# Two weight rings moved to the far end of SBUF, three RWKV tensors moved to the near end

## What is computed

```python
def first_block(x, ...):
    for i in range(2):                       # layer a, layer b
        hn = rms_norm(x, norm_gain[i])
        y = mixer_a(hn, ...) if i % 2 == 0 else mixer_b(hn, ...)
        x = x + y
    return x

def second_block(x, c, ...):                 # one layer
    shift, scale, gate = split(silu(c) @ ada_w + ada_b, 3)
    p = (rms_norm(x, g) * (1 + scale) + shift) @ w_in
    y_a = rwkv7_branch(...)                  # recurrence over 512 tokens, 8 heads
    y_b = dsa_branch(...)                    # top-128 sparse attention, 8 heads
    merged = sigmoid(g_a) * ((y_a * silu(z_a)) @ w_pa) + sigmoid(g_b) * ((y_b * silu(z_b)) @ w_pb)
    return rms_norm(x + gate * (merged @ w_o), final_g)
```

## Time and profile before

| what | value |
|---|---|
| median of three runs | 1697.31 us |
| profiled execution, its own time | 1696.8 us |
| its span, first to last instruction | 1695.0 us |
| outside the span | 1.8 us |
| mean granted TensorE clock | 0.971 of 2.4 GHz |
| instructions in the trace | 30316 |

### The profile page before, as it was taken

One profiled execution on the slowest core, in us unless ns is written; L12 is line 12 of the kernel. 1 busy time (PEld: TensorE's weight loads), 2 busy tenths in 40 slices (PEclk: granted clock), 3 DMA queues, 4 the chain that ended last, 5 costly groups with the idle time before them and its releaser, 6 DMA issues. The chain is left out here.

```text
span 1695.0 us, 30316 instructions
## 1 busy us (share of the span) xinstructions
PE 1574.4 (93%) x12050; PEld 1287.3 (76%) x12050; DVE 813.9 (48%) x1662; ACT 766.4 (45%) x1407; POOL 784.2 (46%) x472
## 2 busy tenths in 40 slices
PE   6899999999999998889999988999978998899997
PEld 4788888888888886667777766676757886688876
DVE  4224243433434344435655534179436754575535
ACT  4544536363545534346556543245664343232222
POOL 4734426162534423365555443425647651365651
PEclk9999999999999999999999998999988999799999
DMA  7413222232323220354444213432000000333331
GB/s 180 125 51 99 78 80 88 69 110 66 105 73 90 73 79 8 94 137 145 143 134 134 79 33 86 119 71 73 26 27 3 3 4 15 87 100 99 88 91 59
DMA packets 247188, 136.60 MB, mean 81 GB/s; under 512 B 24390, under 2 KB 241518, under 8 KB 246999
## 3 DMA queue, kind: packets, MB, share of 16 engines
q1 hardware_dynamic: 220824, 109.19, 23.4%
q10 hardware_dynamic: 26224, 25.47, 5.3%
HBM read 132.11 MB, written 2.52 MB: 79 GB/s over the span
## 5 line engine op out<-in xcount | busy, mean ns | idle before, releaser
L318 PE MATMUL a_proj<-h_low,w_high 128*128 128x512 f32 x472 | 190.3, 403 | 1.5 <-POOL h_low L931 0.8
L912 POOL TENSOR_TENSOR a_sq_low<-a_sq,a_sq_high 128x512 fp32r<-128x512 f32 x48 | 62.0, 1292 | 278.2 <-ACT a_sq_high L764 278.2
L892 POOL TENSOR_TENSOR w_low<-a_w_raw,w_high 128x1024 fp32r<-128x1024 f32 x64 | 158.2, 2472 | 66.2 <-ACT w_high L731 66.2
L320 PE MATMUL a_proj<-h_high,w_high 128*128 128x512 f32 x472 | 185.6, 393 | 0.0
L319 PE MATMUL a_proj<-h_high,w_low 128*128 128x512 f32 x472 | 184.4, 391 | 0.0
L892 POOL TENSOR_TENSOR w_low<-b_w_raw,w_high 128x1024 fp32r<-128x1024 f32 x40 | 103.3, 2584 | 100.9 <-ACT w_high L731 100.9
L318 PE MATMUL b_proj<-h_low,w_high 128*128 128x512 f32 x288 | 116.2, 403 | 1.4 <-POOL h_low L931 0.8
L320 PE MATMUL b_proj<-h_high,w_high 128*128 128x512 f32 x288 | 113.7, 395 | 0.0
L319 PE MATMUL b_proj<-h_high,w_low 128*128 128x512 f32 x288 | 112.7, 391 | 0.0
L812 ACT ACTIVATE a_pt<-a_turned 128x512 f32<-128x512 f32 x64 | 37.8, 591 | 153.8 <-PE a_turned L610 153.8
L318 PEld LDWEIGHTS a_proj<-h_low,w_high 128*128 128x128 f32 x472 | 88.8, 188 | 22.8 <-DVE a_qk L962 3.2
(11 more groups left out here) (451 smaller groups left out, 4300.5 us busy)
## 6 DMA issues: line engine op xcount, KB each, us to landing
a_w_raw<-in_a_w_in_dram SPq DMA_DIRECT2D x78, 512.0 KB, 3.8
b_w_raw<-in_b_w_in_dram SPq DMA_DIRECT2D x30, 512.0 KB, 4.2
b_ada_w<-in_ada_w_dram ACTq DMA_DIRECT2D x24, 512.0 KB, 3.6
f_wt<-in_w_in_dram SPq DMA_DIRECT2D x22, 512.0 KB, 3.7
a_bias<-scr_a ACTq DMA_DIRECT2D x16, 576.0 KB, 4.6
sparse_w_raw<-in_w_in_dram SPq DMA_DIRECT2D x17, 512.0 KB, 4.1
a_w_raw<-in_a_w_out_dram SPq DMA_DIRECT2D x8, 512.0 KB, 3.7
b_w_raw<-in_b_w_out_dram SPq DMA_DIRECT2D x8, 512.0 KB, 3.8
```

The costliest lines, as they stand in the source:

```text
L318: nc.tensor.matmul(out, lh, rl, start=first, stop=False)
L320: return nc.tensor.matmul(out, lh, rh, start=False, stop=last)
L892: nc.gpsimd.tensor_tensor(low(slot_of(b)), raw[:, n % RAW, :, :], high(slot_of(b)), ALU.subtract).then_inc(s_wl, 1)
L912: nc.gpsimd.tensor_tensor(sql[:, :], sq[:, u % 2, :], sqh[:, :], ALU.subtract).then_inc(s_sql, 1)
```

## The change

The two rings are taken from the right side and are opened right behind `edge`, ahead of all that is given out from the left after `h_low`. Since `ring` is the same helper, the rings of `merge` move to the right side as well. The three RWKV tensors, which were on the right, are taken from the left. Nothing else is edited.

```diff
--- before.py
+++ after.py
@@ -2740,6 +2740,9 @@
 
         T.HH, T.HL = (ctx.enter_context(nc.sbuf_tensor(n, [P, KT, SEQ], F32R)) for n in ("h_high", "h_low"))
         ctx.enter_context(nc.sbuf_tensor("edge", [P, LINE // 2], F32, side="right"))
+        rings = ctx.enter_context(ExitStack())
+        ring = lambda name, slots: rings.enter_context(nc.sbuf_tensor(name, [P, slots, KT, P], F32R, side="right"))
+        T.wh, T.wl = ring("w_high", RING), ring("w_low", RING)
         T.slot0 = 0
         T.pair_ones_r = ctx.enter_context(nc.sbuf_tensor("pair_ones_r", [P, P], F32R))[:, :]
         T.eps = sb("eps", [P, LINE])
@@ -2748,9 +2751,6 @@
         T.mod_lines = sb("mod", [P, 2 * LINE])
         T.mod, T.wi = T.mod_lines[:, 0:MODS], sb("wi", [P, 2 * LINE])
         T.causal = part("causal")
-        rings = ctx.enter_context(ExitStack())
-        ring = lambda name, slots: rings.enter_context(nc.sbuf_tensor(name, [P, slots, KT, P], F32R))
-        T.wh, T.wl = ring("w_high", RING), ring("w_low", RING)
 
         a, b = layer_a(T, I), layer_b(T, I)
         w_in = I["w_in_2"][0].rearrange("(k p) n -> p k n", p=P)
@@ -2762,8 +2762,8 @@
         retire(nc, T)
         attention_layer(nc, T, I, b)
         retire(nc, T)
-        with nc.sbuf_tensor("rwkv_in", [P, C_SHIFTED, SEQ], F32, side="right") as rw, \
-                nc.sbuf_tensor("rwkv_w", [P, 512], F32, side="right") as T.rwl, nc.sbuf_tensor("rwkv_vec", [P, 8, 4], F32, side="right") as T.rvec:
+        with nc.sbuf_tensor("rwkv_in", [P, C_SHIFTED, SEQ], F32) as rw, \
+                nc.sbuf_tensor("rwkv_w", [P, 512], F32) as T.rwl, nc.sbuf_tensor("rwkv_vec", [P, 8, 4], F32) as T.rvec:
             T.rw = rw
             with nc.sbuf_tensor("sparse_in", [P, C_TILES - C_SHIFTED, SEQ], F32) as sp_in, \
                     nc.sbuf_tensor("sparse_table", [P, 8, 512], F32) as T.table, \
```

## The result

| | before | changed |
|---|---|---|
| runs | 10 | 10 |
| median | 1703.66 us | 1712.49 us |
| lowest to highest | 1696.8 to 1708.46 | 1710.18 to 1715.86 |
| profiled execution, its own time | 1696.8 us | 1709.94 us |

The changed kernel is slower: ratio 1.0058, 95% interval 1.0045 to 1.0072. That ratio is about 10 us; the two medians of the table lie 8.8 us apart. The ten runs of before have a median 6 us above that of the three shown at first. So the loss is small, and it is real.

What follows compares the result with a forecast made beforehand. PE's rate was taken to bound five of six stages. All terms summed to 0 on the profiled 1696.8 us, forecast 1697 us; small terms of 6.5 us and the highest run shown, 1708.5, gave the range 1690 to 1709.

Steps and rivals of the forecast that it cites:

- What bounds the kernel: Whole kernel: PE's rate prices five of six stages, busy 93% of the span; `recurrent` by latency of short instructions.
- Weights read by PE: 3696 matmuls with ring weights moving from 87104 to beyond 200000: taken as 0, bound 18.5 us either way.
- the two 273s: Turning `a_probs` at 215616 and `b_probs` at 165440 takes 273 ns each; cited against a cost of far weights.
- The 5 ns bound: Largest difference in one matmul form, 394 ns with `h_low` against 389 with `f_y_low`; on 3696 matmuls 18.5 us either way.
- The slower rival: Ring weights read from the far end of SBUF cost PE up to 5 ns a matmul: 1715.5 us, chance 6%.
- The faster rival: PE gains 5 ns a matmul because the rings no longer lie right behind `h_low`: 1678.5 us, chance 6%.
- The small terms: Port hold-ups 3.5 us, DMA remainders 1.7, ACT and DVE addresses in `recurrent` 1.3: each taken as 0, together 6.5 either way.
- the 3.5 us: PE's wait for one of POOL's 104 low halves in layers a and b, taken as the hold-up term's bound.
- The transfers' rival: Modulated stage's first weights land 1.7 us later through their remainder by 256, and PE waits: 1699 us, chance 8%.
- The 22% more for the sparse blocks: DMA estimate: a 512-byte row takes 18 beats from remainder 64 and 22 from 192.
- What I named as signs: If right: PE busy within 0.5% per stage, L318 at 394 ns; slower: 399 or more on L318 to L320; faster: 389.

Runs made afterwards that it cites:

- m1: Matmuls alone, no other engine at work, with weights and moving operand at chosen addresses; 226.7 to 233.6 ns a matmul.
- e1: Changed kernel with 128 bytes more in `edge`, so the rings stay on the right but at remainder 64 by 256; ratio 1.0006.
- e3: Kernel before with 64 bytes ahead of the rings, so rings and left stage tensors stand at remainder 128; ratio 0.998.
- e6: Changed kernel with 64 bytes more in `edge` and 64 ahead of the stage tensors, all at remainder 128; ratio 0.9967, median 1695.12 us.
- e4: Changed kernel with 64 bytes more in `edge`: rings on the right at remainder 128, stage tensors still at 64; ratio 0.9985.
- e5: Changed kernel with 64 bytes ahead of `h_high`, so `h_high` and `h_low` go to remainder 192 like the rings; ratio 1.0001.
- m2: Matmuls alone, weights fixed at remainder 128, moving operand shifted in steps of 16 bytes; 226.7 to 234.5 ns for 512 columns.
- m3: Matmuls alone, even and odd matmuls with their own shifts of weights and moving operand, some with 32 weight columns; 226.7 to 233.4 ns.

## Why the prediction was wrong

**What bounds the kernel** was right: PE's rate sets five of six stages. That is why a few ns in it could reach the end.

**The step that failed is "Weights read by PE", where I took 0.** I asked only how far the weights move, and picked the pair `merge_w_high` and `f_w_high` as the nearest rows. Both stand at remainder 64, so the pair shows that distance is free (m1 and e1 confirm it) and could not show what the change alters. The other pair, the two 273s of `a_probs` and `b_probs`, is blind in the same way: 215616 and 165440 also both stand at 64. I had the remainders in hand, and weighed them for ACT and for DMAs, where they cost nothing, but not for PE's two operands against each other. What the runs show in its place: the difference went from 64 to 192, and a matmul from 229 to 233 ns. (In `merge` the products on `y` and on the merged tensor, 13 of the 154 blocks, went from 0 to 128, with 228.6 and 233.1 ns on `y`.)

**The 5 ns bound was the clue.** 394 ns with `h_low` against 389 with `f_y_low`, both with weights at 64: I said that I did not know whether it was the address. It was: `h_low` has difference 64, `f_y_low` difference 0. With `h_low` at difference 0 the same row reads 389 (e3, e6). But as a price the 5 ns meant nothing. They are a difference of listed durations, whose ends are modelled. In distances the `f_y` blocks of before average 228.6 ns against 229.0 for `h` with the same weights, since at each change of operand they need up to ten matmuls to settle at 226.7.

**The size.** By the means of the blocks: layer a 229.7 to 233.1 ns on 64 blocks, 5.2 us; layer b 229.1 to 233.2 on 40, 3.9 us; modulated 228.9 to 233.3 on 6, 0.6 us; sparse 230.2 to 233.4 on 17, 1.3 us; merge 229.0 to 233.3 on 27, 2.8 us. The sum is 13.8 us, or 0.81% of 1697; the two comparisons gave 0.58 and 0.87%. The slower rival had 18.5 us for it, a third too much, and its mechanism, the far end, was wrong. That it came within a third is luck: its 5 ns came from durations, and the durations of `h_low` don't differ between 64 and 192. I also let it decide only from 4.6 ns on, and so gave no room to a slowdown below 1%: the measured 1712.49 us lies 3.5 us above the range. The sample of the kernel before accounts for that much: its ten runs have a median 6 us above the one that I built on, and 1.0058 times 1697.31 would be 1707.2.

**The faster rival** named the wrong cause but a real reserve: PE can have 226.7 instead of 229.1 ns. It took a difference of 0 rather than a greater distance. Its 18.5 us were too many. e3 gives 3.9 us and e6 4.9. Of the 2.4 ns that lie between 229.1 and 226.7, layers a and b show 2.0 and 1.0 ns, since their products are cut short before the rate has settled, and y and merged products had the 0 already.

**The small terms held.** ACT, DVE and POOL kept their durations, and the recurrent stage took 194.9 us against 195.8. One reading under them was wrong: the 3.5 us that PE waited behind L892 were for `a_wv_low`, which the same line writes and whose longest takes 2430 ns. So none of the 104 ring blocks made PE wait, and the 3.5 us in the range had no held-up block behind them. They changed nothing in the outcome. The transfers' rival fell: `sparse_w_raw` lands in 3.6 us at remainder 192, against 4.1 at 64, and `r_next_w_raw` in 5.1 us at 64, against 5.8 at 192 (two transfers). The 22% more for the sparse blocks, the estimate from the Trainium skill (DMA: Bandwidth & Descriptors, section How a descriptor splits into AXI transactions), is not seen here.

**What I named as signs** was only half of use. I expected a slower PE to show as 399 ns on L318, but the listed durations stayed at 394; it showed in the busy time of the windows, which I had also named (at most 0.5%, and it grew by 0.7% in layer a and 2.7% in layer b), and in the starts.

## What to carry to other kernels

When tensors are moved in SBUF, compare the starts of a matmul's two operands by 256 bytes, before and after, and not only how far each moves; here 0 gives 227 ns for 512 float32r columns, and other differences up to 235. (float32r is the kernel's type for the rounded halves; the rows call it f32.) In a kernel that is bound by such products, a filler of 64 or 128 bytes that brings weights and moving tensors to one remainder is worth trying, and costs no memory to speak of. It has to be one remainder for all tensors that share the ring: e4 and e5 mended the products on `h`, spoiled those on `f_y`, and gained 0.15% and nothing, where e6 gained 0.33%. And judge a matmul by the distance of starts in the timeline or by PE's busy time in a window of equal count, since a median duration of 394 ns hid a step from 229 to 233.

## What the runs showed of the hardware that I had not expected

The distance of back-to-back 512-column matmuls depends on the difference of the operands' starts: 226.7 ns at 0, 229.1 at 64, 232.5 at 128, 233.2 at 192, up to 234.5 at 208 (m2). The place doesn't matter, 87104 or 212544, left or right, and busy engines beside PE don't either. 256 bytes are like 0.

The rate also depends on what PE did just before. At difference 0 it takes up to some ten matmuls after a break until the distances are 226.7 ns (e3). At difference 64 there are two rates, 229.0 and 233.3 ns, and a block of 24 matmuls can stay in either from its first to its last (e1, e5). Which one a block takes, and why, is open. The Trainium skill (SBUF — State Buffer, section Who interferes with whom) says that PE never waits on anyone, having one read port for the moving operand and one for the weights. The runs show no engine that would disturb PE, which agrees, but PE alone runs at different rates by where its own two operands start.

A mix of differences from matmul to matmul gives 231.6 ns even where each matmul's own difference is 0, and so do weights of 32 columns at the two steady differences tried, 0 and 192 (m3). Why, is open, and so is what inside PE makes the difference of the starts count at all.
